# A one-core hybrid decoder step: the expert stage as 67 blocks of one expert each, or as 35 turns of a streamed and a resident block

## The chip, the core and the metric

The kernel runs on one core of a Trainium2 chip, in one launch. The metric is the device time of that core in microseconds (us). Everything is computed in float32.

## What is computed

One layer of a decoder: a prompt of 256 tokens and 8 samples of 4 tokens, so 288 tokens of width 1024. Modulation, input projection, dilated attention (the samples over cached keys and values) and a short convolution come first. The change is in the mixture of experts behind them: 32 experts, each token goes to the four with the highest logits, and each expert is a clamped SwiGLU layer with three 1024x1024 matrices.

```python
logits = xt @ w_router + b_router
top_v, top_i = lax.top_k(logits, TOP_K)          # 4 of 32
gates = jax.nn.softmax(top_v, axis=-1)
...
def expert_block(args):
    xblk, e = args
    g = xblk @ w_gate[e] + b_gate[e]
    u = xblk @ w_up[e] + b_up[e]
    g = jnp.minimum(g, SWIGLU_LIMIT)
    u = jnp.clip(u, -SWIGLU_LIMIT, SWIGLU_LIMIT)
    act = (u + 1) * g * jax.nn.sigmoid(SWIGLU_ALPHA * g)
    return act @ w_down[e] + b_down[e]
...
y = segment_sum(yb * row_g[:, None], row_tok)    # gated rows are added to their tokens
```

## The kernel before

Five programs run side by side, one for each engine, and wait for each other by semaphores written out by hand; nothing is scheduled for them. The input projection, attention and output projection use a ring of 12 slots (`ring`), each a weight piece of 128x2048 float32, 1 MB. Router, tables and experts follow.

**Blocks.** The rows that go to one expert are cut into blocks of 32 (`ROWS`). There are always `NB` = 288x4/32 + 31 = 67 blocks, in the order of the experts: each expert has one for every 32 rows begun, and experts with one block get an empty second one while blocks are left. An expert's weights are 12 pieces of 1 MB: four of w_gate (GATE), four of w_up (UP), four of w_down (DOWN). Every expert is loaded once, 384 pieces in all.

**A block on TensorE (PE), `moe_block`.** `biases` starts the sums in banks 0 and 1 with the owning expert's biases; `weights` runs the GATE pieces, then UP, then DOWN. A piece is 8 matmuls of 32 rows by 256 columns, four side by side in the array (16 records of the trace, since float32 makes two of one). Between them stand `combine(b - 1, h)`, which spreads the gated rows of the last block over the 288 token columns in two halves, `gather(b + 1)`, which picks the next block's 32 rows out of `h2tok` by a one-hot matrix, and the transposes `act_rows_T` (L892) and `gather_T` (L862).

**The other engines in a block.** VectorE (DVE) clips gate (L1304) and up (L1308), multiplies gate by its sigmoid (L953, two SBUF operands) and by up (L1316, two SBUF operands), writes the gated one-hot (L1289) and adds each combined half to `acc` (L953, 128x1152, 1.35 us). ScalarE (ACT) does the sigmoid and copies gathered and transposed rows out of PSUM.

**Loading.** All weight DMAs are issued by SyncE (SP) on one queue. UP and DOWN pieces, and expert 0's GATE pieces, go straight into the ring slot of their piece when the last block of the expert before has used it (`weights_used`). GATE pieces of the other experts go into four slots of `stage`, and GpSimd (POOL) copies them into the ring in two halves of 128x1024 (L479, L480), without a wait between the halves. So while one expert is computed, 16 pieces can be loaded or under way: 12 in the ring and 4 in the stage. Expert 0's 12 pieces and expert 1's GATE pieces are loaded during attention and the output projection (`EARLY` and what follows it). TensorE reads the block's expert from a table (`blk_e`).

## Time and profile before

| | us |
|---|---|
| median of 3 runs (1657.16 to 1665.85) | 1664.88 |
| the profiled execution | 1660.6 |
| its span, first to last instruction | 1658.5 |
| PE busy (matmul) | 1462.2 (88%) |
| DVE busy | 522.7 (32%) |
| ACT busy | 245.4 (15%) |
| POOL busy | 260.9 (16%) |
| DMA | 495.72 MB, mean 299 GB/s |
| granted TensorE clock, mean | 0.929 of 2.4 GHz |

The page puts 59% of the chain that ended last on the matmul helper's line L499 and 17% on transfers of w_gate and w_down. The expert blocks run from 428.3 us to about 1638.2 us of the span; the tables are ready at about 408.8 us. Shares of the whole span say little here, since the stages have different limits: in the page's 40 slices DMA stands at 400 GB/s and more in some slices of the expert stage and at 0 in others. "Records" below are the trace's matmul instructions.

### The profile page before, as it was taken

Reading aid. Unit: us, or ns where it says so; the run is one execution under the profiler, and the core shown is the slowest. Engines: PE = TensorE matmul, PEld = TensorE weight load, DVE = VectorE, ACT = ScalarE, POOL = GpSimd, SP = SyncE. Lnnn points to the kernel's source line nnn. Section 1 sums busy time; section 2 is a strip of 40 time slices with the busy share of each in tenths; the row PEclk is TensorE's granted clock in tenths of the full one; section 3 lists DMA queues with packets and bytes.
Section 4 is the critical chain, followed back from the end, with each engine's and each line's share of the span. In section 5 each row is a group of like instructions: output and inputs, shape, how many; then the busy total and the mean of one; then the engine's idle time right before and its main releaser. Section 6 shows DMA issues by size and latency. Waiting matters only on the chain.

```text
span 1658.5 us, 48934 instructions
## 1 busy us (share of the span) xinstructions
PE 1462.2 (88%) x20629; PEld 802.8 (48%) x20630; DVE 522.7 (32%) x1107; ACT 245.4 (15%) x639; POOL 260.9 (16%) x270
## 2 busy tenths in 40 slices
PE   6998999886999999999999997987689996776896
PEld 3885576563445555554555553532245552222353
DVE  2224445335223333333323332321123321121234
ACT  2113433311111111011111110100011110000011
POOL 0000000000211122123103111111300112312110
PEclk9998899897799999999999998988799998777898
DMA  9956989623196999999939969299960569999805
GB/s 338 370 219 227 335 314 344 236 94 127 56 400 250 406 404 401 407 405 399 405 125 382 404 256 410 87 411 409 410 266 0 206 256 409 410 410 409 328 25 207
DMA packets 143136, 495.72 MB, mean 299 GB/s; under 512 B 9069, under 2 KB 26085, under 8 KB 140030
## 3 DMA queue, kind: packets, MB, share of 16 engines
q1 hardware_dynamic: 141902, 491.00, 76.0%
q0 software_dynamic: 1200, 4.23, 0.7%
q8 instruction: 26, 0.43, 0.1%
q14 instruction: 8, 0.07, 0.0%
HBM read 492.22 MB, written 2.97 MB: 299 GB/s over the span
## 4 chain that ended last, share of the span: by engine, by line
PE 63%; DMA 20%; SPq 6%; DVE 5%; issue 3%; ACT 2%; POOL 1%; POOLq 0%; DVEq 0%; ACTq 0%
PE ps L499 59%; DMA arena<-in_w_gate 12%; DMA ring<-in_w_down 5%; SPq L405 5%; DMA arena<-in_cache_k 2%; PE ps L673 1%; PE ps L862 1%; DVE hT L953 1%; ACT hT L1525 1%; SPq L361 1%; POOL ring L480 1%; DVE arena L1289 1%; DVE hT L1308 1%; PE ps L514 0%; PE ps L648 0%
## 5 line engine op out<-in xcount | busy, mean ns | idle before, releaser
L499 PE MATMUL ps<-ring,hT 128*32 128x256 f32 (+2 forms) x13728 | 869.5, 389 | 101.9 <-POOL ring L480 51.7
L499 PEld LDWEIGHTS ps<-ring,hT 128*32 128x32 f32 (+1 forms) x13728 | 464.1, 114 | 471.4 <-issue 89.8
L499 PE MATMUL ps<-arena 128*32 128x258 f32 (+6 forms) x4252 | 258.6, 369 | 24.0 <-ACT arena L1459 3.7
L479 POOL COPY ring<-arena 128x1024 f32<-128x1024 f32 x124 | 129.0, 1040 | 941.1 <-PE ps L499 684.4
L1304 DVE TENSOR_SCALAR hT<-ps 128x256 f32<-128x256 f32 x67 | 28.4, 424 | 648.1 <-PE ps L499 648.1
L499 PEld LDWEIGHTS ps<-arena 128*32 128x32 f32 (+4 forms) x4252 | 129.0, 115 | 137.6 <-issue 93.5
L953 DVE TENSOR_TENSOR arena<-arena,ps 128x1152 f32<-128x1152 f32 x134 | 180.5, 1347 | 30.9 <-PE ps L499 30.9
L480 POOL COPY ring<-arena 128x1024 f32<-128x1024 f32 x124 | 131.3, 1059 | 0.0
L499 PE MATMUL ps<-arena,hT 32*128 32x288 f32 x1072 | 109.2, 478 | 2.0 <-DVE arena L953 1.5
L1525 ACT COPY hT<-ps 128x258 f32<-128x258 f32 x67 | 25.1, 375 | 440.6 <-PE ps L499 314.8
L1534 ACT ACTIVATE hT<-hT 128x256 f32<-128x256 f32 x67 | 27.9, 417 | 395.5 <-DVE hT L1304 395.5
L1308 DVE TENSOR_SCALAR hT<-ps 128x256 f32<-128x256 f32 x67 | 28.4, 424 | 181.3 <-PE ps L499 181.3
L499 PEld LDWEIGHTS ps<-arena,hT 32*128 32x128 f32 x1072 | 44.1, 193 | 64.5 <-issue 61.6
L1542 ACT COPY hT<-ps 128x256 f32<-128x256 f32 x67 | 24.9, 372 | 247.4 <-PE ps L499 247.4
L499 PE MATMUL ps<-hT,ring 128*128 128x288 f32 x224 | 56.5, 416 | 4.5 <-DVE hT L1173 3.4
L673 PE MATMUL ps<-ident,arena 128*128 128x128 f32 x336 | 49.8, 291 | 4.1 <-DMA arena<-in_cache_k 3.6
L499 PEld LDWEIGHTS ps<-hT,ring 128*128 128x128 f32 x224 | 43.5, 195 | 17.2 <-issue 5.0
L1357 ACT COPY arena<-ps 32x64 f32<-32x64 f32 (+6 forms) x91 | 31.7, 356 | 132.8 <-PE ps L499 101.6
L673 PEld LDWEIGHTS ps<-ident,arena 128*128 128x128 f32 x336 | 38.1, 147 | 14.9 <-issue 9.6
L862 PE MATMUL ps<-ident,hT 128*128 128x128 f32 x134 | 29.6, 303 | 13.7 <-ACT hT L1525 7.9
L1101 DVE COPY arena<-ps 128x512 f32<-128x512 f32 x40 | 27.7, 692 | 40.8 <-PE ps L673 40.8
L953 DVE TENSOR_TENSOR hT<-hT 128x256 f32<-128x256 f32 x67 | 39.6, 591 | 0.0
(191 smaller groups left out, 631.7 us busy)
## 6 DMA issues: line engine op xcount, KB each, us to landing
ring<-in_w_up SPq DMA_DIRECT2D x128, 1024.0 KB, 10.1
ring<-in_w_down SPq DMA_DIRECT2D x128, 1024.0 KB, 13.1
arena<-in_w_gate SPq DMA_DIRECT2D x124, 1024.0 KB, 18.1
ring<-in_w_ada SPq DMA_DIRECT2D x24, 1024.0 KB, 8.3
arena<-in_cache_k SPq DMA_DIRECT2D x56, 384.0 KB, 6.8
arena<-in_cache_v SPq DMA_DIRECT2D x56, 384.0 KB, 5.0
ring<-in_w_in SPq DMA_DIRECT2D x12, 1024.0 KB, 12.0
ring<-in_w_out SPq DMA_DIRECT2D x4, 1024.0 KB, 8.6
```

Of the source, the lines that this page charges most:

```text
L405: sp.dma_start(dst, src.rearrange("o (k p) c -> p (o k) c", p=P)).then_inc(signal, 16)
L479: pool.tensor_copy(slot[:, 0:half], stage[:, j, 0:half])
L480: pool.tensor_copy(slot[:, half:], stage[:, j, half:]).then_inc(staged_out, 1)
L499: return te.matmul(out, a, b, start=first, stop=last)
L673: last = tr(ps[:, b + hp // 4, (hp % 4) * P:(hp % 4 + 1) * P], K[:, c, hp * P:(hp + 1) * P], ident[:, :])
L862: last = tr(ps[:, 3, c * P:(c + 1) * P], xrows[:, c * P:(c + 1) * P], ident[:, :])
L953: return ve.tensor_tensor(out, a, b, op)
L1304: ve.tensor_scalar(tg, ps[:, 0, 0:256], LIMIT, None, ALU.min).then_inc(g_clipped, 1)
L1308: ve.tensor_scalar(tu, ps[:, 1, 0:256], LIMIT, -LIMIT, ALU.min, ALU.max).then_inc(u_clipped, 1)
L1357: return step(se.copy(out, in_), signal)
L1525: se.copy(xrows, ps[:, 3, 0:GW]).then_inc(x_copied_rows, 1)
L1534: se.activation(sg, tg, ACT.Sigmoid, scale=ALPHA).then_inc(g_sig, 1)
```

## The change

The 67 blocks become 35 turns (`TURNS`) of two blocks each (`PAIR`), 70 blocks. The first block of a turn is **streamed**: its 12 pieces come through the four stage slots, all twelve, and TensorE reads them there. The second is **resident**: its weights stand in the ring's 12 slots, where GpSimd puts them. GpSimd copies every piece of every turn out of the stage, in two halves. If the streamed expert is "heavy" (over 32 rows), the copy goes into the ring slot of the piece, and this expert's further blocks are the resident ones of this and the next turns. If it is "light", the copy goes to a spare place behind the ring (`SPILL`, 128x1024 float32, in `mem`), by an address computed from a register. Heavy experts are put at the turns where their further blocks begin, light ones at the turns that are left. Each turn streams 12 pieces whatever the routing, 420 in all.

A stage slot is free when TensorE has used it for the streamed block (`piece_used[0]`) and GpSimd has copied it (`held_in`); SyncE waits for both. Each GpSimd copy waits for the one before it (`held_in`). TensorE goes piece by piece: streamed piece j, then resident piece j, and the latter waits for GpSimd's copy of piece j in this turn. Biases, gather, transposes and combine are done for two blocks at a time; `combine` adds both blocks of a turn in PSUM, so the number of 128x1152 additions on VectorE stays two a turn. `actT` goes through banks 4 and 5, which `combine` uses too, so `act_rows_T` waits for the addition (`acc_added`). Nothing is loaded ahead any more: every expert DMA follows the tables. The bias sums of `b_down`, before ahead of the first block, stand inside turn 0. The tables themselves are made by other small steps.

```diff
@@ program, SyncE
-            for j in range(EARLY):
-                sp.wait_ge(pieces_used, FRONT_PIECES - SLOTS + 1 + j)
-                expert_piece(0, j)
...
-            for j in range(EARLY, EXP_PIECES):
-                sp.wait_ge(pieces_used, FRONT_PIECES - SLOTS + 1 + j)
-                expert_piece(0, j)
-            sp.wait_ge(o_copied, 2 * HPS * NSEQ)
-            for j in range(STAGES):
-                expert_piece(1, j)
+            def turn(t):
+                at = exp_row[0:1, t:t + 1] if isinstance(t, int) else exp_row[0:1, ds(t, 1)]
+                e = sp.value_load(at.bitcast(I32), min_val=0, max_val=NEXP - 1)
+                for j in range(EXP_PIECES):
+                    if not isinstance(t, int) or EXP_PIECES * t + j >= STAGES:
+                        sp.wait_ge(piece_used[0], EXP_PIECES * t + (j - STAGES + 1))
+                        sp.sem_inc(wait_passed, 1)
+                        sp.wait_ge(held_in, 2 * EXP_PIECES * t + 2 * (j - STAGES + 1))
+                        sp.sem_inc(wait_passed, 1)
...
+                    sp.dma_start(stage[:, j % STAGES, :].rearrange("p (k c) -> p k c", c=D),
+                                 src.rearrange("o (k p) c -> p (o k) c", p=P)).then_inc(stage_in[j % STAGES], 16)
@@ GpSimd
-                for j in range(STAGES):
-                    pool.wait_ge(stage_in[j], 16 * e)
-                    pool.wait_ge(weights_used, before * EXP_PIECES + (j + 1))
...
-                    pool.tensor_copy(slot[:, 0:half], stage[:, j, 0:half])
-                    pool.tensor_copy(slot[:, half:], stage[:, j, half:]).then_inc(staged_out, 1)
+                for j in range(EXP_PIECES):
+                    pool.wait_ge(stage_in[j % STAGES], 48 * t + 16 * (j // STAGES + 1))
+                    if not isinstance(t, int) or t > 0:
+                        pool.wait_ge(piece_used[1], EXP_PIECES * t + (j - EXP_PIECES + 1))
+                    for h in range(2):
+                        if not isinstance(t, int) or t > 0 or j > 0 or h > 0:
+                            pool.wait_ge(held_in, 2 * EXP_PIECES * t + (2 * j + h))
+                        pool.sem_inc(wait_passed, 1)
+                        home = j * PIECE + h * SPILL
+                        pool.tensor_copy(mem[:, ds(light * (SLOTS * PIECE - home) + home, SPILL)],
+                                         stage[:, j % STAGES, h * SPILL:(h + 1) * SPILL]).then_inc(held_in, 1)
@@ TensorE
+            def piece(b, j, i, x, bank):
+                if i == 0:
+                    te.wait_ge(stage_in[j % STAGES], 48 * b + 16 * (j // STAGES + 1))
+                    W = stage[:, j % STAGES, :].rearrange("p (k c) -> p k c", c=D)
+                else:
+                    te.wait_ge(held_in, 2 * EXP_PIECES * b + 2 * (j + 1))
+                    W = slot_w(j, rows=True)
...
+            def turn(b, first=False, last=False):
...
+                biases()
+                for u, pieces in enumerate((GATE, UP)):
+                    for j in pieces:
+                        for i in range(PAIR):
+                            piece(b, j, i, xe, 2 * u)
+                    if first:
+                        bias_sums(u)
+                    else:
+                        combine(b - 1, u)
...
+                        gather(b + 1, i)
...
+                    act_rows_T(b, i)
...
+                        gather_T(b + 1, i)
+                for j in DOWN:
+                    for i in range(PAIR):
+                        if j == DOWN[0]:
+                            te.wait_ge(actT_ready, 2 * b + (i + 1))
+                        piece(b, j, i, actT, 4)
@@ VectorE, in turn(b)
+                for i in range(PAIR):
+                    ve.wait_ge(glu, 2 * b + (i + 1))
+                    ve.wait_ge(u_clipped, 2 * b + (i + 1))
+                    ve.scalar_tensor_tensor(tu[i], tu[i], 1.0, sg[i], ALU.add, ALU.mult).then_inc(act_ready, 1)
+                total(b, 1, first)
                 gated_rows(b)
```

How the instructions stand, first on GpSimd in the loop over experts before. `ISA` and `REGISTER_ALU` are register steps; pure semaphore steps are not printed.

```order
24 L474 REGISTER_ALU
25 L475 ISA [waits stage_in0]
26 L479 COPY ring<-arena 128x1024 [waits weights_used]
27 L480 COPY ring<-arena 128x1024
28 L475 REGISTER_ALU [waits stage_in1]
29 L479 COPY ring<-arena 128x1024 [waits weights_used]
30 L480 COPY ring<-arena 128x1024
```

And on GpSimd in the loop over turns of the changed kernel, the first piece and the head of the second (a turn has twelve such).

```order
77 L466 ISA [waits stage_in0]
78 L469 REGISTER_ALU [waits piece_used1]
79 L472 ISA [waits held_in]
80 L472 COPY mem<-arena 128x1024
81 L469 REGISTER_ALU
82 L472 ISA [waits held_in]
83 L472 COPY mem<-arena 128x1024
84 L466 REGISTER_ALU [waits stage_in1]
85 L469 REGISTER_ALU [waits piece_used1]
```

Eight copies an expert became 24 a turn, and between any two of them there is now a wait for the earlier one and a register step for the address.

TensorE before, from the end of a block's UP pieces to its first DOWN piece:

```order
484 L499 MATMUL ps<-ring,hT 32x256 [waits piece_in11]
485 L499 MATMUL ps<-ring,hT 32x256 x7
486 L900 REGISTER_ALU
487 L499 MATMUL ps<-arena,hT 128x288 [waits acc_added]
488 L499 MATMUL ps<-arena,hT 128x288 x3
489 L851 ISA
490 L499 MATMUL ps<-arena 32x258 [waits hot_ready]
491 L499 MATMUL ps<-arena 32x258 x11
492 L892 MATMUL ps<-ident,hT 128x128 [waits act_ready]
493 L892 MATMUL ps<-ident,hT 128x128
```

The same place in a turn of the changed kernel (`arena` in a weight matmul is the stage, `mem` the ring):

```order
530 L499 MATMUL ps<-mem,hT 32x256 [waits held_in]
531 L499 MATMUL ps<-mem,hT 32x256 x7
532 L900 REGISTER_ALU
533 L499 MATMUL ps<-arena,hT 128x288 [waits acc_added]
534 L499 MATMUL ps<-arena,hT 128x288 x7
535 L847 ISA
536 L849 REGISTER_ALU [waits hot_ready]
537 L499 MATMUL ps<-arena 32x259 [waits u_clipped]
538 L499 MATMUL ps<-arena 32x259 x11
539 L499 MATMUL ps<-arena 32x259 [waits u_clipped]
540 L499 MATMUL ps<-arena 32x259 x11
541 L888 REGISTER_ALU
```

The stretch has twice the matmuls, its last UP piece waits for GpSimd instead of for a DMA, and the first transpose behind it (row 542 of that list) waits for `acc_added` and `act_ready`.

## Rows read from the trace of the kernel before

**Rows 1.** Two stretches: us, busy us (count) by engine, PEclk, DMA share, GB/s.
```profile
1140.00:1171.00 31.00, 21.69 (x252) 8.44 (x252) 5.07 (x10) 1.86 (x5) 8.34 (x9) 0.78 1.03 410
1235.00:1296.00 61.00, 60.50 (x1011) 31.85 (x1006) 19.59 (x40) 7.49 (x20) 0.00 (x0) 1.00 0.00 0
```

**Rows 2.** Timeline of PE over a block with no wait: start us, us, instruction.
```profile
1233.16 3.66 PE L499 MATMUL ps<-ring,hT 128*32 128x256 f32 x64
...
1241.78 3.66 PE L499 MATMUL ps<-ring,hT 128*32 128x256 f32 x64
1245.37 0.77 PE L499 MATMUL ps<-arena,hT 32*128 32x288 f32 x8
1246.06 1.51 PE L499 MATMUL ps<-arena 128*32 128x258 f32 x24
1247.51 0.44 PE L892 MATMUL ps<-ident,hT 128*128 128x128 f32 x2
...
1248.48 1.72 PE L499 MATMUL ps<-ring,hT 128*32 128x256 f32 x28
```

**Rows 3.** DMA issues of L405 in the stretch 351 to 375.3 us, each alone in its queue.
```profile
DMA to landing us min/median/max: 4.7/4.8/4.9
```

**Rows 4.** Chain of waits, from a landed stage piece to its copy, and from PE's use to the next DMA.
```profile
1107.27 0.02 issue
1107.30 0.03 POOLq L475
1107.33 0.04 issue
1107.37 0.02 POOLq L476
1107.39 0.11 issue
1107.51 0.06 POOL ring L479
...
1109.58 1.89 PE ps L499 x16
1111.47 0.08 SPq L405
...
1111.85 2.12 SPq L405
```

**Rows 5.** Timeline: two VectorE steps under GpSimd's copies, then the copies of one piece.
```profile
484.63 1.04 POOL L479 COPY ring<-arena 128x1024 f32<-128x1024 f32 x1 [0.47 <-DMA arena<-in_w_gate]
484.70 1.24 DVE L953 TENSOR_TENSOR hT<-hT 128x256 f32<-128x256 f32 x1
485.61 1.23 POOL L480 COPY ring<-arena 128x1024 f32<-128x1024 f32 x1
485.98 1.14 DVE L1316 SCALAR_TENSOR_TENSOR hT<-hT 128x256 f32<-128x256 f32 x1
...
1168.94 1.04 POOL L479 COPY ring<-arena 128x1024 f32<-128x1024 f32 x1 [0.54 <-DMA arena<-in_w_gate]
...
1169.93 1.04 POOL L480 COPY ring<-arena 128x1024 f32<-128x1024 f32 x1
...
1171.02 1.51 PE L499 MATMUL ps<-ring,hT 128*32 128x256 f32 x12 [0.62 <-POOL ring L480]
```

**Rows 6.** Timeline of VectorE between two blocks' UP and DOWN pieces, no copy running.
```profile
1245.50 0.42 DVE L1308 TENSOR_SCALAR hT<-ps 128x256 f32<-128x256 f32 x1 [2.15 <-PE ps L499]
1245.84 0.42 DVE L953 TENSOR_TENSOR hT<-hT 128x256 f32<-128x256 f32 x1
1246.30 0.42 DVE L1316 SCALAR_TENSOR_TENSOR hT<-hT 128x256 f32<-128x256 f32 x1
1246.64 0.43 DVE L1289 TENSOR_SCALAR arena<-arena,hT 128x288 f32<-128x288 f32 x1
...
1247.06 1.34 DVE L953 TENSOR_TENSOR arena<-arena,ps 128x1152 f32<-128x1152 f32 x1
```

**Rows 7.** Timeline at the start of the expert stage.
```profile
413.97 4.20 PE L499 MATMUL ps<-arena 32*128 32x288 f32 x8 [1.68 <-DVE arena L1268]
...
423.76 0.20 PEld L499 LDWEIGHTS ps<-arena 128*32 128x32 f32 x8 [0.76 <-issue]
...
426.63 0.37 ACT L1525 COPY hT<-ps 128x258 f32<-128x258 f32 x1 [17.01 <-PE ps L499]
...
428.31 1.11 PE L499 MATMUL ps<-arena 32*32 32x256 f32 x16 [0.55 <-ACT hT L1529]
...
429.35 8.37 PE L499 MATMUL ps<-ring,hT 128*32 128x256 f32 x128
```

**Rows 8.** Chain of waits at the end of the expert stage.
```profile
1637.08 1.11 PE ps L499 x16
...
1638.22 0.38 ACT hT L1542
...
1641.72 1.36 DVE arena L953
```

More of the change, by code:

```diff
@@ L838, in _, with gather @@
+                last = mm(ps[0:tn, 5, 256 + NB * t:256 + NB * (t + 1)], GT[0:NEXP, t0:t0 + tn], own2[0:NEXP, :], True, True)
             step(last, places_T)
-            te.wait_ge(place_ready, 3)
-            for h in range(2):
+            def gather(b, i):
+                if i == 0:
+                    te.wait_ge(hot_ready, 2 * b + 2)
+                if not isinstance(b, int) or b > 0:
+                    te.wait_ge(u_clipped, 2 * b + (i - 1))
+                for t in range(3):
+                    for q in range(4):
+                        last = mm(ps[q * 32:(q + 1) * 32, 2 + i, 0:GW], hot[:, t, i * ROWS:(i + 1) * ROWS], h2tok[:, t, q, :],
+                                  t == 0, t == 2)
+                last.then_inc(x_made, 1)
@@ new lines, in biases, with act_rows_T @@
+            def biases():
+                for q in range(4):
+                    for i in range(PAIR):
+                        for u in range(2):
+                            r = slice((2 * i + u) * NEXP, (2 * i + u + 1) * NEXP)
+                            mm(ps[32 * q:32 * q + 32, 2 * u + i, 0:256], own_b[r, :], brow[r, q * 256:(q + 1) * 256], True, False)
+            def act_rows_T(b, i):
+                te.wait_ge(act_ready, 2 * b + (i + 1))
+                if i == 0:
+                    te.wait_ge(acc_added, 2 * b + 2)
+                for c in range(2):
+                    last = tr(ps[:, 4 + i, c * P:(c + 1) * P], tu[i][:, c * P:(c + 1) * P], ident[:, :])
+                last.then_inc(act_T, 1)
@@ new lines, in combine @@
+            def combine(b, h):
+                if h == 0:
+                    te.wait_ge(ye_ready, 2 * b + 2)
+                    te.wait_ge(hotg_ready, 2 * b + 2)
+                te.wait_ge(acc_added, 2 * b + 2 + h)
+                for i in range(PAIR):
+                    for q in range(4):
+                        last = mm(ps[:, 4 + q, 0:NT], ye[i][32 * q:32 * q + 32, h * P:(h + 1) * P], hotg[i][32 * q:32 * q + 32, :],
+                                  i == 0, i == 1)
+                last.then_inc(comb_made, 1)
@@ L909, in moe_block @@
-            def moe_block(b, first=False, last=False):
-                at = blk_e[0:1, b:b + 1] if isinstance(b, int) else blk_e[0:1, ds(b, 1)]
-                e = te.value_load(at.bitcast(I32), min_val=0, max_val=NEXP - 1)
-                te.wait_ge(xe_ready, b + 1)
+            for i in range(PAIR):
+                gather(0, i)
+            for i in range(PAIR):
+                gather_T(0, i)
+            def turn(b, first=False, last=False):
+                te.wait_ge(xe_ready, 2 * b + 2)
@@ new lines, in turn @@
+                for i in range(PAIR):
+                    ve.wait_ge(g_sig, 2 * b + (i + 1))
+                    TT(sg[i], sg[i], tg[i], ALU.mult).then_inc(glu, 1)
+                total(b, 0, first)
+                for i in range(PAIR):
+                    ve.wait_ge(piece_used[i], EXP_PIECES * b + 8)
+                    if not first:
+                        ve.wait_ge(act_T, 2 * b + (i - 1))
+                    ve.tensor_scalar(tu[i], ps[:, 2 + i, 0:256], LIMIT, -LIMIT, ALU.min, ALU.max).then_inc(u_clipped, 1)
@@ new lines, in copy_x, with turn @@
+            def copy_x(b):
+                for i in range(PAIR):
+                    se.wait_ge(xT_made, 2 * b + (i + 1))
+                    se.copy(xe[i], ps[:, 2 + i, 0:256]).then_inc(xe_ready, 1)
+            def turn(b, first=False, last=False):
+                for i in range(PAIR):
+                    se.wait_ge(g_clipped, 2 * b + (i + 1))
+                    if not first:
+                        se.wait_ge(act_ready, 2 * b + (i - 1))
+                    se.activation(sg[i], tg[i], ACT.Sigmoid, scale=ALPHA).then_inc(g_sig, 1)
@@ L1544, in _ @@
             copy_rows(0)
             copy_x(0)
-            moe_block(0, first=True)
-            with se.Fori(1, NB - 1) as b:
-                moe_block(b)
-            moe_block(NB - 1, last=True)
+            turn(0, first=True)
+            with se.Fori(1, TURNS - 1) as b:
+                turn(b)
+            turn(TURNS - 1, last=True)
             load_sqrt()
```

397 lines of the change are left out of this document (177 added, 220 removed).

## The prediction

> **What bounds the kernel now.** I read the rates of stretches first, then the timeline of one block, then the chain of waits. A block that waits for nothing takes 15.32 us of TensorE, from the first DOWN matmul at 1233.16 to the next block's at 1248.48 [rows 2]; 67 of them would be 1026 us. The expert stage, from 428.31 to 1638.19 us, takes 1210 [rows 7, 8]. The 184 us between are waits for weights. They fall where experts have one block each: between 1140 and 1171 us DMA runs at 410 GB/s, TensorE holds 252 matmul records in 31 us and its granted clock averages 0.78 of 2.4 GHz. Where one expert has many blocks it is the other way: from 1235 to 1296 us DMA moves nothing and TensorE holds 1011 records in 61 us at clock 1.00 [rows 1]. So two resources take turns at being the bound. A piece of 1.049 MB takes 2.56 us at 410 GB/s, an expert's twelve 30.7 us, two blocks 30.6 us. The change lays the two side by side; at best a turn would cost 30.7 us and 35 turns 1075 us. The question is what a turn really costs.
>
> **The period of a turn.** Four stage slots set a loop. Next turn's GATE piece 0 needs the slot of this turn's DOWN piece 0, and TensorE reads DOWN piece 0 only after the long gap between UP and DOWN. I follow this loop from the moment F when GpSimd ends the last copy of UP piece 3.
>
> - TensorE starts the resident UP piece 0.05 us after that copy (the copy ends at 1170.97, TensorE starts at 1171.02) [rows 5]. The piece costs 0.90 us, a quarter of the 3.59 us between 1241.78 and 1245.37 [rows 2]. F + 0.95.
> - `combine` was 0.69 us, 1245.37 to 1246.06 [rows 2]. With twice the records it costs between 0.69 and 1.38; I take 1.2, since the switch between shapes is paid once. F + 2.15.
> - Two gathers at 1.45 us each, 1246.06 to 1247.51 [rows 2]: F + 5.05.
> - The transposes of one block and what they wait for took 0.97 us, 1247.51 to 1248.48 [rows 2], two blocks' between 0.97 and 1.94: DOWN begins at F + 6.0 to 7.0. VectorE may be later than that: from F + 1.05 on it has a clip (0.42), two products, which took 0.42 each alone and 1.14 to 1.24 while GpSimd copied, the addition (1.34), and two gated one-hots (0.43) before ScalarE may copy rows and then `actT` (0.38 each) [rows 5, 6, 8]. With one product free and one held that is 1.05 + 0.42 + 0.42 + 1.14 + 1.34 + 0.86 + 0.76 = 6.0, with both held 6.8. I take F + 6.5.
> - The streamed DOWN piece 0 ends 1.1 us later [rows 8], SyncE's steps up to the issue took 0.38 us (1111.47 to 1111.85) [rows 4], and a DMA alone in its queue took 4.7 to 4.9 us to land [rows 3]: F + 12.8. During the gap the four DOWN pieces fill the slots, DMA stands still for some 2 to 3 us, and nothing later gives them back.
> - From landing to GpSimd's copy 0.24 us (1107.27 to 1107.51) [rows 4]: F + 13.0.
> - Then sixteen copies for GATE and UP. A copy took 1.04 us [rows 5]. Before, the second half began 0.99 us after the first; now each waits for the one before. No row of before shows such a wait on GpSimd. Its pieces are there: 0.05 us until a waiter sees the copy's end [rows 5], 0.02 + 0.11 us from the semaphore step to the copy, 0.03 us for a register step and 0.04 behind it [rows 4]. That is 0.27 us with the gaps, so 1.31 us a copy. The bounds are 1.24 (the address step hidden) and 1.45 (it costs several such steps). 16 x 1.31 - 0.27 = 20.7: F + 33.7.
> - VectorE's steps with two SBUF operands hold GpSimd up in return: a copy with such a step ahead took 1.23 us, 0.19 more [rows 5]. Three fall among these sixteen copies (two gate products, the one-hot): 0.6.
>
> The period is **34.3 us**: more than DMA's 30.7, and more than GpSimd's 24 x 1.31 = 31.4. TensorE itself has about 29 us of work in it (six times 3.6 for weights, then 2.4, 2.9, 2 and under 1 for biases), so it isn't the bound.
>
> The Trainium skill, "SBUF — State Buffer", section "Who interferes with whom", says that a VectorE instruction with two SBUF inputs and a GpSimd instruction that reads SBUF exclude each other for a whole instruction. The trace agrees, with 1.24 against 0.42 us for one product [rows 5, 6]; without that rule's cost the period would be about 33.3, by the same rows.
>
> **Start and end.** Attention doesn't change: the loads taken out of it were issued where the queue was waiting for TensorE. The tables take about as many steps as before, so I leave 413.97 as the moment when they stand [rows 7]; the small added steps, 0.2 us each, are about balanced by dropped ones. The bias sums (413.97 to 423.76) move into turn 0, where loading covers them. Then 0.4 for the one-hot, two gathers at 2.87 (423.76 to 426.63, low clock), 2.4 for copies and transposes of two blocks (1.68 for one), twice 1.04 for biases, and 1.9 for GATE piece 0 at the low clock: 426.5 [rows 4, 7]. The first four pieces have landed by then. UP piece 0 is issued and lands 5.2 later, and four pieces of copies (0.24 + 8 x 1.31 - 0.27) end at about 442: this is F of turn 0. With expert 0 no longer loaded ahead, this fill is the price at the front. After the last F: DOWN begins about 5.5 later (no gather), its eight pieces take 7.2, the tail from 1638.19 to the end of the span took 20.3 [rows 8] and has two longer combines, 0.5 each: 34.0.
>
> Sum: 442 + 34 x 34.3 + 34.0 = 1642 us of span, against 1658.5. The profiled execution was 2.1 us over its span and the median of the runs 4.3 us over that, so the median after should be **1648 us**, 1.0% less. Each 0.1 us of the period is 3.4 us of time. The time is unchanged at a period of 34.8; faster by over 0.5% below 34.5, slower by over 0.5% above 35.0 (about what a measurement of this kernel can tell from no change).
>
> **Rivals.**
>
> *Loading sets the pace (0.24).* If the copies go at 1.24 us, eight landings at 2.56 us rule: 12.8 + 17.9 + 0.24 + 2.45 = 33.4, and 32.9 with the shortest gap. The time would be 442 + 34 x 33.2 + 34 + 6.4 = 1611 us. For it: the copies' bound is only 5% away. Against it: sixteen copies are then within 0.1 us of loading, with VectorE pushing them.
>
> *GpSimd's copies cost more, slower than before (0.25).* If a dependent copy with a register address costs 1.45 us, sixteen cost 22.9 and the period is 36.5: 1723 us. It decides from 1.36 us a copy on, since 13.0 + 16 x 1.36 - 0.27 + 0.6 = 35.1. For it: no row shows such a copy, 24 of them follow one another, and VectorE now has five two-operand steps a turn in place of two a block. Against it: the steps visible in rows 4 are short.
>
> *The clock falls (0.05).* Between 1140 and 1171 us the clock averaged 0.78 while TensorE held 8.1 records a us [rows 1]. Were the gap between UP and DOWN at 1.2 GHz, combine, gathers, transposes and DOWN piece 0 would cost twice, some 6 us more: a period of 40 and about 1850 us. Against it: a turn has 504 records in 34.3 us, 14.7 a us, much nearer to the 16.6 of the stretch at 1.00. The Trainium skill, "TensorE: Matmul & The Clock Gate", Part 1, says that the clock is throttled by default and released by activity; that waiting lowers it agrees with the 0.78 here.
>
> *The change does all it says (0.04).* If the stage covered the gap, a turn would cost 30.7 us: 442 + 34 x 30.7 + 40.4 = 1526 us. Against it stands the loop above: the slot isn't free.
>
> **How the numbers follow.** The forecast has 0.42; its own range is a period of 33.8 to 34.9, 1632 to 1669 us. About 0.25 of it lies on the faster side of 0.5%, 0.11 within and 0.06 beyond. With the rivals: faster 0.25 + 0.24 + 0.04 = 0.53, within 0.5% 0.11, rounded to 0.12, slower 0.06 + 0.25 + 0.05, so 0.35. The range leaves out the full cover, the low clock and the dear end of the copies: 1598 to 1715 us.
>
> **What would show it.** Twelve pieces every 34.3 us, DMA at about 370 GB/s with one pause a turn, at the GATE pieces; GpSimd copies starting 1.31 us apart in GATE and UP, idle for about 2 us before GATE piece 0; TensorE's resident pieces released by GpSimd; clock 1.00 through the turns. Wrong would be: copies over 1.36 us apart, a chain that runs through GpSimd without passing the DMA of GATE piece 0, or a first F later than 445 us.

## The result, and the profile after

The changed kernel took 1671.35 us (median of 20 runs, 1661.08 to 1685.33), the kernel before 1658.98 (20 runs, 1653.78 to 1671.55): ratio 1.0065, 95% interval 1.0046 to 1.0083. The forecast was 1648 and "faster". The time lies in the range, on the other side of no change.

The page of the kernel after: span, clock, transfer rate, the chain that ended last, and the group of GpSimd's copies.

```profile
span 1671.0 us, 54045 instructions
...
PEclk9998899997999999999999999999999999999998
...
GB/s 337 371 213 238 122 320 347 217 24 74 327 369 369 370 330 363 369 368 365 331 370 361 363 360 350 342 371 353 364 371 309 351 370 357 368 359 345 366 366 158
...
POOL 40%; PE 23%; DMA 19%; issue 8%; DVE 4%; POOLq 4%; SPq 1%; ACT 1%; DVEq 0%; ACTq 0%
...
L472 POOL COPY mem<-arena 128x1024 f32 x840 | 899.3, 1071 | 408.1 <-POOL mem L472 195.6
```

TensorE's granted clock is 0.99 of 2.4 GHz on the mean of the turns, where it had averaged 0.78 in the loading stretches [rows 1], and DMA runs from the first turn to the last, at 357 GB/s on the mean (row below). So the change did what its structure says. F, the end of UP piece 3's copies, is at 438.98 us in turn 0 and at 1637.07 in turn 34: 34 periods of 35.24 us. Two stretches of the kernel after (us, busy us (count) by engine, clock, DMA share, GB/s), the standstill in one turn, and all turns:

```profile
973.20:976.20 3.00, 3.00 (x54) 1.80 (x58) 0.00 (x0) 1.01 (x4) 2.49 (x3) 1.00 0.15 36
...
438.98:1637.07 1198.09, 1015.02 (x17128) 527.28 (x17128) 305.45 (x508) 116.74 (x340) 874.54 (x818) 0.99 0.92 357
```

One turn, whose F is at 966.85. First TensorE's timeline (start us, us, instruction, wait ahead), which answers to [rows 2]: resident UP piece 3, combine, gathers, transposes, then DOWN, streamed (`arena`) and resident (`mem`) by turns.

```profile
966.90 1.07 PE L499 MATMUL ps<-mem,hT 128*32 128x256 f32 x16 [0.65 <-POOL mem L472]
967.90 1.25 PE L499 MATMUL ps<-arena,hT 32*128 32x288 f32 x16
969.08 2.83 PE L499 MATMUL ps<-arena 128*32 128x259 f32 x48
...
973.16 0.44 PE L860 MATMUL ps<-ident,arena 128*128 128x128 f32 x2 [0.44 <-ACT arena L1561]
973.53 1.07 PE L499 MATMUL ps<-arena,hT 128*32 128x256 f32 x16
974.41 1.05 PE L499 MATMUL ps<-mem,hT 128*32 128x256 f32 x16
```

Then VectorE between the same pieces, which answers to [rows 6], with ScalarE's copy of the second gather's rows, which waits for the one-hots; and SyncE's issues of the next GATE pieces:

```profile
968.38 1.59 DVE L1354 SCALAR_TENSOR_TENSOR mem<-mem 128x256 f32<-128x256 f32 x2
969.89 1.34 DVE L971 TENSOR_TENSOR arena<-arena,ps 128x1152 f32<-128x1152 f32 x1
971.16 1.48 DVE L1318 TENSOR_SCALAR arena<-arena 128x288 f32<-128x288 f32 x2
972.73 0.38 ACT L1561 COPY arena<-ps 128x259 f32<-128x259 f32 x1 [0.75 <-DVE arena L1318]
```
```profile
975.01 5.48 SPq L426 DMA_DIRECT2D arena<-in_w_gate  x4
```

Last GpSimd's copies from the end of DOWN on, which answer to [rows 5]:

```profile
976.72 1.04 POOL L472 COPY mem<-arena 128x1024 f32 x1 [0.25 <-POOL mem L472]
980.25 1.04 POOL L472 COPY mem<-arena 128x1024 f32 x1 [2.49 <-DMA arena<-in_w_gate]
981.55 1.04 POOL L472 COPY mem<-arena 128x1024 f32 x1 [0.26 <-POOL mem L472]
983.52 1.04 POOL L472 COPY mem<-arena 128x1024 f32 x1 [0.93 <-DMA arena<-in_w_gate]
984.81 1.04 POOL L472 COPY mem<-arena 128x1024 f32 x1 [0.25 <-POOL mem L472]
...
991.27 1.04 POOL L472 COPY mem<-arena 128x1024 f32 x1 [0.25 <-POOL mem L472]
992.57 1.30 POOL L472 COPY mem<-arena 128x1024 f32 x1 [0.25 <-POOL mem L472]
```

And the chain of waits for GATE 1, from its issue over its landing to its first copy:

```profile
976.78 6.34 DMA arena<-in_w_gate
...
983.15 0.03 POOLq L466
...
983.22 0.03 POOLq L469
...
983.30 0.02 POOLq L470
...
983.38 0.06 POOLq L472
...
983.51 0.03 POOLq L469
983.54 1.03 POOL mem L472
```

The loop of the prediction is all there. DOWN begins 6.7 us behind F in this turn, and on the median of the turns too. GATE 0 is issued at 8.2 and first copied at 13.4, after an idle 2.49 us. Copies then follow 1.29 us apart (1.04 and a pause of 0.25). The row that the forecast doesn't have is the one at 983.52: GpSimd stands idle a second time, 0.93 us, for GATE 1, whose load took 6.34 us.

### The profile page after: what moved, and what is told of

It is laid out like the page before. It is cut to its first block, busy times and chain, and to the rows that moved or that the text cites. A ratio compares the mean times of both kernels' runs of the same rounds, so it can differ in the third digit from the quotient of the medians.

```text
span 1671.0 us, 54045 instructions
## 1 busy us (share of the span) xinstructions
PE 1410.4 (84%) x21389; PEld 804.2 (48%) x21389; DVE 488.1 (29%) x970; ACT 241.7 (14%) x654; POOL 910.3 (54%) x864
## 4 chain that ended last, share of the span: by engine, by line
POOL 40%; PE 23%; DMA 19%; issue 8%; DVE 4%; POOLq 4%; SPq 1%; ACT 1%; DVEq 0%; ACTq 0%
POOL mem L472 40%; PE ps L499 20%; DMA arena<-in_w_gate 14%; DMA arena<-in_cache_k 2%; POOLq L472 2%; DMA arena<-in_w_up 2%; PE ps L673 2%; DVE arena L971 1%; SPq L372 1%; POOLq L469 1%; DVE arena L1318 1%; POOLq L470 1%; DMA arena<-in_w_down 0%; PE ps L514 0%; PE ps L648 0%
## 5 line engine op out<-in xcount | busy, mean ns | idle before, releaser
L472 POOL COPY mem<-arena 128x1024 f32 x840 | 899.3, 1071 | 408.1 <-POOL mem L472 195.6
L499 PE MATMUL ps<-mem,hT 128*32 128x256 f32 (+2 forms) x7584 | 522.1, 372 | 171.0 <-POOL mem L472 168.8
L499 PE MATMUL ps<-arena,hT 128*32 128x256 f32 (+1 forms) x7840 | 530.7, 389 | 5.7 <-DMA arena<-in_w_gate 3.3
L499 PEld LDWEIGHTS ps<-mem,hT 128*32 128x32 f32 (+1 forms) x7584 | 257.4, 113 | 401.4 <-POOL mem L472 283.2
L499 PEld LDWEIGHTS ps<-arena,hT 128*32 128x32 f32 (+1 forms) x7840 | 258.1, 121 | 205.6 <-issue 64.9
L499 PE MATMUL ps<-arena 128*32 128x259 f32 (+5 forms) x4376 | 220.6, 360 | 17.8 <-ACT arena L1493 3.7
L499 PEld LDWEIGHTS ps<-arena 128*32 128x32 f32 (+3 forms) x4376 | 121.6, 112 | 102.1 <-issue 55.0
L971 DVE TENSOR_TENSOR arena<-arena,ps 128x1152 f32<-128x1152 f32 (+1 forms) x71 | 94.1, 1325 | 10.5 <-PE ps L499 10.4
L499 PE MATMUL ps<-hT,mem 128*128 128x288 f32 x224 | 56.5, 416 | 4.5 <-DVE hT L1191 3.4
L1354 DVE SCALAR_TENSOR_TENSOR mem<-mem 128x256 f32<-128x256 f32 x70 | 53.9, 812 | 0.0
```

The source lines that it names most:

```text
L472: pool.tensor_copy(mem[:, ds(light * (SLOTS * PIECE - home) + home, SPILL)], stage[:, j % STAGES, h * SPILL:(h + 1) * SPILL]).then_inc(hel ...
L499: return te.matmul(out, a, b, start=first, stop=last)
L971: return ve.tensor_tensor(out, a, b, op)
L1354: ve.scalar_tensor_tensor(tu[i], tu[i], 1.0, sg[i], ALU.add, ALU.mult).then_inc(act_ready, 1)
```

## The experiments

The period is the distance from the F of turn 0 to that of turn 34, over 34. Columns: median (the two kernels with half of the copies have one run), ratio to the kernel before with its interval, period, and, behind F on the mean of 32 turns, when GATE 0 is issued and first copied.

| kernel | median us | ratio | period | issue | copy |
|---|---|---|---|---|---|
| after | 1671.35 | 1.0065 [1.0046, 1.0083] | 35.24 | 8.15 | 13.50 |
| e1 half of the copies | 1597.63 | | 33.25 | | |
| e2 streamed DOWN first | 1648.75 | 0.9917 [0.9892, 0.9941] | 34.37 | 8.17 | 13.52 |
| e3 combine early | 1614.68 | 0.9716 [0.9666, 0.9766] | 33.60 | 6.19 | 11.83 |
| e4 e3, streamed DOWN 0 ahead | 1636.65 | 0.9851 [0.9808, 0.9894] | 34.03 | 4.41 | 11.63 |
| e5 e2 and e3 | 1578.75 | 0.9509 [0.9485, 0.9533] | 32.57 | 6.19 | 11.55 |
| e6 e4 in another order | 1603.03 | 0.9671 [0.9643, 0.9698] | 33.06 | 4.70 | 11.79 |
| e7 e6, half of the copies | 1525.50 | | 30.83 | | |
| e8 e6, half loads | 1583.77 | 0.9564 [0.9539, 0.9588] | 32.60 | 4.22 | 11.37 |
| e9 e5, half loads | 1583.05 | 0.9558 [0.9526, 0.9591] | 32.61 | 6.23 | 11.18 |
| e10 gathers in UP | 1578.90 | 0.9535 [0.9510, 0.9560] | 32.55 | 5.93 | 11.22 |
| e11 e5, two spill places | 1554.51 | 0.9381 [0.9352, 0.9410] | 31.77 | 6.19 | 11.56 |
| e12 e10, two spill places | 1570.97 | 0.9479 [0.9449, 0.9510] | 32.18 | 6.55 | 10.71 |
| e13 e11, half loads | 1556.79 | 0.9368 [0.9314, 0.9422] | 31.91 | 6.23 | 10.70 |

**e1, half of the copies.**
```diff
-                    for h in range(2):
+                    for h in range(1):
```


> The kernel after, but GpSimd copies only the first half of each piece (12 copies a turn in place of 24), so the resident block works with half of its weights left over from other data; loads, matmuls and waits are otherwise the same. The trace of after has a mean turn of 35.24 us from one end of the copies of UP's last piece (F) to the next. Theory A, the four-slot loop: the stretch from F to GATE0's landing (13.3 us) stays, since it goes through the combine, the gathers, the transposes and the first DOWN piece and holds no copy; behind it the pieces GATE0 to UP3 then come in at the pace of their loads, about 2.75 us each, 7 x 2.75 = 19.3, and one copy with its gap (1.3) ends the turn, less a few tenths that no longer collide: 33.3 us a turn, and a span of 439 + 34 x 33.3 + 34 = 1605 us. Theory B, GpSimd's 24 copies of a turn are themselves the bound, and the wait before GATE0 only looks like a cause: with 12 copies the turn falls to TensorE's own work, 30.7 us, and the span to about 1517 us. Theory C, the bare pace of the loads is the bound already: no change, 1671 us.

(The counts that SyncE, GpSimd and TensorE wait for are halved with it.) Measured: span 1595.7, period 33.25. GpSimd's copy count is halved and the period falls by 2 us only. GpSimd in one turn of e1:

```profile
944.19 1.04 POOL L472 COPY mem<-arena 128x1024 f32 x1 [3.09 <-DMA arena<-in_w_gate]
947.75 1.04 POOL L472 COPY mem<-arena 128x1024 f32 x1 [2.52 <-DMA arena<-in_w_gate]
950.26 1.04 POOL L472 COPY mem<-arena 128x1024 f32 x1 [1.47 <-PE ps L499]
952.82 1.04 POOL L472 COPY mem<-arena 128x1024 f32 x1 [1.52 <-PE ps L499]
```

From GATE 1 on the copies come 2.56 us apart, the pace of the loads at 410 GB/s. (TensorE, named as releaser, had used the place of that copy a turn before; the wait that ended last is the load.) In after two copies take 2.59. So loads and copies were about 1% apart behind GATE 1, and the stretch from F to GATE 0's copy, 13.3 us here and 13.5 in after, stays. Theory A holds; B would have had 30.7 and C no change. Its terms were others, though: not seven pieces at 2.75 us, but 3.4 us to GATE 1's copy and six at 2.56.

**e2, the streamed DOWN pieces first.**
```diff
-                for j in DOWN:
-                    for i in range(PAIR):
+                for i in range(PAIR):
+                    te.wait_ge(actT_ready, 2 * b + (i + 1))
+                    for j in DOWN:
```


> The kernel after, but TensorE takes the four streamed DOWN pieces first and the four resident ones after them, in place of one and one by turns; nothing else changes. In after GATE's loads are issued 1.78 us apart (8.16, 9.94, 11.64, 13.27 us behind F), because each waits for two DOWN pieces of TensorE; GATE1's copy starts 3.3 us behind GATE0's, where two copies take 2.58. Theory A: the issues of GATE1 to GATE3 come 0.9 us apart, GATE1 lands within the 2.6 us of GATE0's copies, the 16 copies from GATE0 to UP3 run without that pause, and the turn falls by 0.7 us to 34.5: span 439 + 34 x 34.5 + 34 = 1646 us, ratio to the kernel before about 0.992. Rival: four loads asked for almost at once share the queues, GATE0's landing is put off by what GATE1 gains, and the turn stays at 35.2: 1671 us.

Measured: 1648.75 us, 34.37 a turn. SyncE's four issues of GATE in a turn of e2, and GpSimd's copies:

```profile
937.32 3.38 SPq L426 DMA_DIRECT2D arena<-in_w_gate  x4
```
```profile
942.63 1.04 POOL L472 COPY mem<-arena 128x1024 f32 x1 [2.55 <-DMA arena<-in_w_gate]
943.93 1.04 POOL L472 COPY mem<-arena 128x1024 f32 x1 [0.26 <-POOL mem L472]
945.22 1.04 POOL L472 COPY mem<-arena 128x1024 f32 x1 [0.25 <-POOL mem L472]
```

The four issues take 3.38 us, where in after they took 5.48, and the second wait is gone: GATE 1's copy starts 2.59 us behind GATE 0's in nearly every turn, in place of 3.41 on the mean. GATE 0's isn't put off (13.52). The order in which the two blocks read DOWN cost 0.87 us a turn.

**e3, the combine early.** TensorE does `combine(b - 1, 1)` behind UP piece 1; VectorE its `total` and `gated_rows` before UP's clips.
```diff
-                    if first:
-                        bias_sums(u)
-                    else:
-                        combine(b - 1, u)
+                        if j in (GATE[3], UP[1]):
+                            if first:
+                                bias_sums(u)
+                            else:
+                                combine(b - 1, u)
...
                 total(b, 0, first)
+                total(b, 1, first)
+                gated_rows(b)
```


> The kernel after, but the second half of the previous turn's combine stands behind UP's second piece in place of behind its last, and VectorE does its sum and the gated one-hots ahead of UP's clips. TensorE's work between F and the first DOWN piece loses 1.2 us. Theory A, the four-slot loop runs through that stretch: DOWN0 begins 1.2 us earlier (5.3 us behind F in place of 6.5), so does GATE0's load, GpSimd's wait for it falls by 1.2 us, and the turn falls from 35.2 to 34.0: span 439 + 34 x 34.0 + 34 = 1629 us, ratio to the kernel before 0.982. Theory B or C (copies or the pace of the loads alone): no change, since all the work is still there, 1671 us.

Measured: 1614.68 us, 33.60, more than expected. GATE 0 is issued 1.96 us earlier, not 1.2: the sum and the one-hots (1.34 and 1.48 in the rows of after) had held ScalarE's copy of the gathered rows, and with it the transposes of x, too. TensorE in a turn of e3, with no wait behind resident UP 3:

```profile
912.44 1.07 PE L499 MATMUL ps<-mem,hT 128*32 128x256 f32 x16 [0.33 <-POOL mem L472]
913.33 2.81 PE L499 MATMUL ps<-arena 128*32 128x259 f32 x48
916.07 0.66 PE L892 MATMUL ps<-ident,mem 128*128 128x128 f32 x4
916.56 0.60 PE L860 MATMUL ps<-ident,arena 128*128 128x128 f32 x4
917.09 1.07 PE L499 MATMUL ps<-arena,hT 128*32 128x256 f32 x16
```

**e4, streamed DOWN 0 ahead of the gathers.**
```diff
                         for i in range(PAIR):
+                            if j == UP[3] and i == 1:
+                                act_rows_T(b, 0)
                             piece(b, j, i, xe, 2 * u)
...
+                piece(b, DOWN[0], 0, actT, 4)
                 if not last:
                     for i in range(PAIR):
                         gather(b + 1, i)
+                act_rows_T(b, 1)
+                piece(b, DOWN[1], 0, actT, 4)
```


> The change of e3, and with it the streamed block is carried through on its own: VectorE makes its product ahead of the resident block's clip, TensorE transposes it before the resident UP3 piece and takes the streamed DOWN0 piece ahead of the gathers and the streamed DOWN1 piece behind them; the resident block's transposes, the gathers' transposes and the rest follow. DOWN0 is then used about 1 us behind F in place of 7.6, and the load of GATE0 waits only for GpSimd's copy of DOWN0 (2.6 us behind F). Theory A: the slot loop is no longer the longest one and the pace of the loads sets the turn, 12 x 2.77 = 33.2 us: span about 439 + 34 x 33.2 + 34 = 1602 us, ratio to before 0.966. Theory B (GpSimd's copies are a bound of their own at 24 x 1.29 = 31 us, or longer where VectorE's steps lie over them): at most the same, it can't be told apart from A unless the turn stays above 34. Theory C: 1671 us, no change.

A miss: 34.03, worse than e3. TensorE in a turn of e4:

```profile
918.75 1.05 PE L499 MATMUL ps<-arena,hT 128*32 128x256 f32 x16
921.69 0.44 PE L892 MATMUL ps<-ident,mem 128*128 128x128 f32 x2 [1.90 <-DVE mem L1359]
922.06 1.07 PE L499 MATMUL ps<-mem,hT 128*32 128x256 f32 x16
922.95 1.05 PE L499 MATMUL ps<-arena,hT 128*32 128x256 f32 x16
923.81 2.81 PE L499 MATMUL ps<-arena 128*32 128x259 f32 x48
```

The transposes wait 1.90 us for the product, and resident UP 3, which could run from F on (920.07 in this turn), stands behind them until 922.06; over 1040 us that wait sums to 52.0 us. GATE 0 was issued at 4.4 and not 2.6, and GATE 1 at 8.5, behind both gathers. Of the 1.8 us by which GATE 0 is issued earlier than in e3, 0.2 are left at its first copy (11.63 against 11.83). An engine that executes in order pays for an early place of a step that isn't ready.

**e5, e2 and e3 together.** The diffs of both.

> The two edits of e2 and e3 together: the combine's second half behind UP's second piece, and the four streamed DOWN pieces ahead of the resident ones. In e3 GATE0's first copy starts 11.7 us behind F (13.5 in after) and GATE1's 3.3 us behind it; in e2 that pause is gone (2.59). Theory A, the slot loop with GpSimd's 16 copies at its end: both gains add, GATE0's copy at 11.8 and 16 copies in 20.7 us give a turn of 32.5 us and a span of 439 + 34 x 32.5 + 34 = 1578 us, ratio to before 0.951. Rival: the loads have a floor of their own near 33 us a turn (e1, with half of the copies, ended at 33.25): 439 + 34 x 33.2 + 34 = 1602 us. The records speak for 2.56 us a piece, 30.7 us a turn, which would leave theory A its room.

Measured: 1578.75 us; 32.57 a turn. The gains add (0.87 + 1.64 = 2.51, measured 2.67), and no floor near 33 us shows.

**e6, the order of e4 mended.** Resident UP 3, transposes of block 0, gather, streamed DOWN 0 and 1, gather, transposes of block 1, and the rest.

> The pieces of e4 in another order on TensorE, with VectorE and ScalarE as in e4: resident UP3, transposes of the streamed product, gather of the first block, streamed DOWN0 and DOWN1, gather of the second block, transposes of the resident product, streamed DOWN2, the gathers' transposes, resident DOWN0, streamed DOWN3, resident DOWN1 to DOWN3. In e4 TensorE stood before the resident UP3 piece until VectorE had clipped and multiplied the streamed block, and streamed DOWN1 came only behind both gathers, so GATE0's load was asked for at 4.3 us and GATE1's at 8.4 us behind F. Theory A: here DOWN0 is used 3.5 us behind F and DOWN1 4.4, DOWN1's load has landed by then, so GATE0 is asked for at 3.9 us and GATE1 at 5.2, the queues never run dry, and the turn is set by GpSimd's own 24 copies, 31.0 us and some tenths of collisions: 31.5 us, span 439 + 34 x 31.5 + 34 = 1544 us (0.931). Rival: TensorE, with 30.7 us of work in a turn, is now the late engine wherever it waits once for a product or a copy, and gives 1 to 2 us of that back, as in e4: 32.5 to 33.5 us, 1578 to 1612 us.

A miss on the time, the rival: 33.06. TensorE's wait for the product is down to 13.0 us in 1040, but GATE 0, issued at 4.7, is copied at 11.8 only, and the loads run at 381 GB/s with nothing standing still.

**e7, e6 with half of the copies.** The diff of e1 on e6.

> The kernel of e6 with the edit of e1: GpSimd copies only the first half of each piece, so the resident block works in part with left-over weights. It tells which engine bounds e6. If GpSimd's copies bound e6, the turn falls to the loads' and TensorE's floor, 30.7 us, and the span to 1517 us. If TensorE's waits for products bound e6, it gains only what shorter copies give on the way (1.3 us for the one copy behind UP3): about 1 us a turn less than e6.

Measured: 1525.50 us, 30.7 in nearly every turn (30.83 with the first): 12 loads at 2.56. TensorE's order doesn't bound e6; GpSimd's copies and the slots that they hold do.

**e8, half loads on e6.** Each piece is loaded in two halves with a signal each, and a half is asked for when the half in its place is copied.
```diff
-                        sp.wait_ge(held_in, 2 * EXP_PIECES * t + 2 * (j - STAGES + 1))
+                            sp.wait_ge(held_in, 2 * EXP_PIECES * t + 2 * (j - STAGES) + h + 1)
```


> The kernel of e6, but each piece is loaded in two halves of 512 KB with a signal each, and a half is asked for as soon as GpSimd has copied the half that lay there (SyncE still waits for TensorE once a piece). In e6 nothing runs dry any more, yet the turn is 33.06 us where the loads alone need 12 x 2.56 = 30.7 and GpSimd alone 24 x 1.295 = 31.1. Theory S, the slots: with one of four slots held for 2.6 us by its two copies, at most three loads are on the way; a load behind two others takes 3 x 2.56 = 7.7 us, and a slot's round is 7.7 + 2.6 + 0.4 + waits = 10.8 us, three rounds a turn 32.3 to 33. With halves 3.5 pieces are on the way, the round shrinks by 1.3 us, and the turn falls to GpSimd's 31.4: span 439 + 34 x 31.4 + 34 = 1541 us. Theory T, TensorE's own waits for products set the turn of e6: no change, 1596 to 1603 us.

Measured: 1583.77 us, 32.60, every turn but the first at 32.6. No load is waited for any more, but a copy now also waits for its own half's signal, behind the wait for its predecessor, and the pause grew:

```profile
902.70 1.04 POOL L475 COPY mem<-arena 128x1024 f32 x1 [0.28 <-POOL mem L475]
904.02 1.04 POOL L475 COPY mem<-arena 128x1024 f32 x1 [0.28 <-POOL mem L475]
...
908.09 1.04 POOL L475 COPY mem<-arena 128x1024 f32 x1 [0.39 <-POOL mem L475]
```

24 copies of 1.04 are 25.0 us, 23 pauses of 0.28 (five of 0.33) 6.7, the head of the turn 0.4 and copies lengthened by VectorE 0.5: 32.6. This is GpSimd alone as the bound. The slots' share of e6 was real (nothing waits for a load now), its worth was 0.5 us before the next bound.

**e9, half loads on e5.** The diff of e8 on e5.

> The kernel of e5 with the half loads of e8. In e5 GATE0 is asked for 6.2 us behind F, its first copy starts at 11.5 to 11.6, and 16 copies of 20.7 us follow: 32.5 us. Here the first copy needs only the first half of GATE0's load; estimated from the records, a 1 MB load alone takes 4.8 us and 2.56 us of that is its bytes at the pace of the queues, so half of it takes 4.8 - 1.3 = 3.5. Slot loop: the first copy starts 1.3 us sooner, but GpSimd's eight DOWN copies end only at 10.6, so the turn falls from 32.5 to GpSimd's own 31.4: 1541 us, ratio to before 0.929. Rival: twice as many loads cost SyncE and the queues more than they give (24 x 0.4 us of issue, a pause between loads), and the turn stays at 32.5 or rises: 1579 us or more.

Measured: 1583.05 us, 32.61: nearly the same bound. The first copy comes 0.37 us earlier than in e5, but most pauses are 0.03 us longer and five are 0.08 us longer. The expectation priced the extra wait at nothing.

**e10, gathers in UP.** On the kernel of e8, with its half loads and its order of DOWN.
```diff
+                        if j == UP[2] and not last:
+                            for i in range(PAIR):
+                                gather(b + 1, i)
```


> The half loads of e8 and the early combine of e3, and the gathers of the next blocks are moved too: behind UP's third piece, into the two banks that GATE's sums have left, with their copies by ScalarE; behind F remain resident UP3, the transposes, and DOWN, whose first streamed piece then begins about 2.6 us behind F in place of 4.7. Theory A: GATE0 is asked for by 4 us behind F, nothing but GpSimd's copies is left in the loop, 31.4 us a turn, 1541 us, the same as e9 if that reaches the floor; if e9 doesn't reach it, this one is nearer. Rival: TensorE has nothing left to do while it waits for the products (clip, product, transposes, copy: some 1.5 us), so its own 29.6 us of work and this wait give 31.1 us with no slack, and the turn comes out at 32 us or more: 1561 us.

Measured: 1578.90 us, 32.55. The gathers now stand before UP 3 on TensorE: in one turn streamed UP 3 starts 1.25 us behind F and resident UP 3 2.1. Moving 2.8 us of work out of one gap put it ahead of the pieces that open the next. GATE 0 is issued at 5.93, not 4. That isn't what sets this turn, though: of 1040 us GpSimd waits 3.7 us for loads and 2.8 us for TensorE, and its 24 copies with pauses of 0.28 to 0.33 us fill the turn as in e8. That pause is what the expectation's 31.4 us left out.

**e11, two places for the spilled copies.** With one place each spilled copy writes what the copy before it wrote, so it waits for that one. With two, by turns, it waits for the copy before the last.
```diff
-                            pool.wait_ge(held_in, 2 * EXP_PIECES * t + (2 * j + h))
+                            pool.wait_ge(held_in, 2 * EXP_PIECES * t + (2 * j + h) - 1)
...
-                        pool.tensor_copy(mem[:, ds(light * (SLOTS * PIECE - home) + home, SPILL)],
+                        pool.tensor_copy(mem[:, ds(light * (SLOTS * PIECE + h * SPILL - home) + home, SPILL)],
```


> The kernel of e5, but what GpSimd copies for light experts goes to two places by turns in place of one (four small tiles of VectorE and ScalarE move to make room), so a copy waits for the copy before the last, which has long ended, and no longer for its predecessor. Work, loads and order are the same. In after as in e5 a copy of 1.04 us is followed by 0.25 us in which GpSimd waits for its own signal; in e8 to e10, with one more wait per copy, that pause is 0.28 to 0.33 and the turn stands at 32.5 us although no load and no matmul is waited for. Theory G, this pause is a part of the bound: it falls by 0.15 to 0.2 us, 16 copies from GATE0 on take about 18 us in place of 20.7, but then they wait for the loads, 2.56 us a piece: 11.5 + 7 x 2.56 + 2.3 = 31.7 us a turn, span 439 + 34 x 31.7 + 34 = 1551 us, ratio to before 0.935. Rival: the pause is GpSimd's own start-up of a copy (its address is read from a register) and not the wait: it stays, and so does the turn, 32.5 us, 1579 us.

Measured: 1554.51 us, 31.77. GpSimd in a turn of e11, and its chain:

```profile
936.54 2.02 POOL L477 COPY mem<-arena 128x1024 f32 x2 [1.32 <-DMA arena<-in_w_gate]
939.05 2.02 POOL L477 COPY mem<-arena 128x1024 f32 x2 [0.48 <-DMA arena<-in_w_gate]
941.61 2.02 POOL L477 COPY mem<-arena 128x1024 f32 x2 [0.54 <-DMA arena<-in_w_gate]
```
```profile
DMA 56%; PE 20%; issue 8%; POOL 7%; DVE 3%; POOLq 2%; SPq 2%; ACT 1%; DVEq 0%; ACTq 0%
```

Two copies in 2.02 us: the pause was wholly the wait for the own signal, and its 0.25 us is gone, start-up and address step included. Copies now start 2.56 us apart, at the pace of the loads, and the chain, 40% GpSimd in after, is 56% DMA. 11.56 + 7 x 2.56 + 2.1 = 31.6.

**e12, the same on e10** (so with half loads).

> The same edit on the kernel of e10, in which GATE0's load is asked for early and nothing but GpSimd's copies bounds the turn (32.5 us = 24 copies of 1.32 and 0.8 us at the head of a turn). Theory G: with a pause of about 0.1 us they need 24 x 1.14 + 0.8 = 28.2 us, and the loads bound the turn at 12 x 2.56 = 30.7 us, as in e7: span 439 + 34 x 30.8 + 34 = 1520 us, ratio 0.916. Rival (the pause is GpSimd's start-up): no change, 32.4 us a turn, 1577 us.

A miss: 1570.97 us, 32.18. The pause is gone as a bound, but TensorE is still late at UP 3, GATE 0 is issued at 6.55, and the records of the queues show 277 to 361 GB/s from 7 to 13 us behind F.

**e13, half loads on e11.**

> The kernel of e11 with the half loads of e9. In e11 a turn is 11.5 us from F to GATE0's first copy and then 7 pieces at the pace of the loads and two copies, 31.6 us. The stretch from GATE0's issue (6.2 us behind F) to its first copy, 5.3 us in after and in e2, e5 and e11, is a term of the sum that came out 0.3 us too small. If it is the whole load that the copy waits for, half a load frees the first copy about 1 us sooner: 10.6 us behind F (e9's was held by GpSimd's DOWN copies, which in e11 end at 10.1), then 15 half pieces at 1.28 us and one copy of 1.04: 30.9 us a turn, span 439 + 34 x 30.9 + 34 = 1524 us, ratio to before 0.919. If most of the 5.3 us is a fixed delay of a load and not its bytes, the first copy stays at 11.2 or later and the turn at 31.5: 1545 to 1555 us.

Measured: 1556.79 us, 31.91. The first copy did move, from 11.56 to 10.70 behind F: the half load lands 4.21 us after its issue where the whole one took 4.97, and the copy follows 0.26 us later in place of 0.40. So the load's bytes count in this term. The turn didn't follow: the second half is copied 1.5 us behind the first and the third 1.7 behind that, and the records of the queues show 266 to 376 GB/s from 7 to 13 us behind F, where e11 has 351 to 421 from 8 on. From 8 us on the other kernels with half loads dip too (at the lowest 266 GB/s in e8, 218 in e9, 194 in e10, 283 in e12). What slows eight small loads there stays open.

## Why the prediction was wrong

*The parts that held.* The bound was the one named: from F through the gap, the slot of DOWN 0 and the load of GATE 0 to sixteen copies. e3 and e5 shortened this loop and moved the time; e1 halved the copies and did little. F of turn 0 came at 439.0 (forecast 442), the end at 33.9 (34.0), DOWN at 6.7 (6.5), GATE 0's issue at 8.15 (8.0), the clock at 0.99 (1.00), a copy with its pause at 1.295 us (1.31). All four rivals fell: dependent copies don't come 1.45 us apart, loading alone didn't rule, the clock stood, and a turn costs 35.2 us and not 30.7. So the time did rise, but not by the rival that had it rise.

*The step that failed* is "then sixteen copies for GATE and UP". It took GATE 0's landing as the last wait of a turn and let the copies run through. Its own rule, a slot is asked for when TensorE has read the piece in it, holds for GATE 1 too. From the end of one streamed DOWN piece to the end of the next TensorE reads two pieces (1.78 us), so GATE 1 is issued 1.8 us behind GATE 0. It then takes 6.6 us to land on the mean, where GATE 0's load took 4.95. GpSimd is idle for it for 0.93 us in the turn shown, 0.68 more than its usual pause, and 0.82 more on the mean. The forecast said "one pause a turn"; there are two. e2 takes that order away alone, GATE 1's load takes 6.6 us there too, and the pause is gone: 34.37 us a turn, the forecast's 34.3. That its 1648.75 us also meet the forecast's 1648 is partly luck, since two terms outside the period were off and partly cancel: in e2's profile the F of turn 0 came at 446.2, where the forecast had 442, and the 6.4 us below weren't there.

One thing about this pause stays open. GATE 1 is issued 9.4 to 10.1 us behind F in all of the 32 turns, yet its load takes anything from 5.6 to 7.8 us, and GpSimd is idle for 0.25 to 2.2 us. With a load of 4.8 us, as the forecast had it for GATE 0, there would have been no pause. What makes this load longer, and by another amount in each turn, no run here tells.

*The terms that were mis-sized, and cancel.* A period of 35.16 (mean of turns 2 to 33) against 34.3:

| term | forecast | measured |
|---|---|---|
| F to GATE 0's issue | 7.98 | 8.15 |
| issue to first copy | 5.04 | 5.35 |
| sixteen copies | 20.7 | 16 x 1.295 - 0.25 = 20.47 |
| VectorE's collisions | 0.6 | 0.26 |
| GATE 1's pause | none | 0.82 |
| other waits | none | 0.1 |

The 5.35 are a load of 4.95 (forecast 4.8, from loads alone in their queue [rows 3]) and 0.40 from its landing to its copy (0.24, from a chain with two small steps of GpSimd's sequencer [rows 4], where there are now five, as the chain for GATE 1 shows). e2, with the next load 0.9 us behind in place of 1.8, shows the same 5.35. A copy that VectorE holds up costs more than the 0.19 put down, 1.30 in place of 1.04 at 992.57, but in the turn shown it is the only one of the sixteen, where the forecast had three.

*The front and the offset.* 34 x 0.94 = +32 us for the period and -3 for the start give the span: 1671.0 against 1642. The forecast then added 6.4 us for the distance from span to median, 4.3 of them from three runs whose median lay above the profiled one. Over 20 runs before's median is 0.5 us above its span; that term was 6 us too much and hid a part of the miss.

*The chances.* The forecast wrote that the time rises by over 0.5% from a period of 35.0 on, 0.7 us from its centre, and gave its own case 0.06 on that side. A sum of ten terms with one unexamined wait among them doesn't have that precision.

*Where the gain of the change went.* A turn has 30.7 us of loads and about as much of TensorE's work, yet takes 35.2. 1.6 us are the combine, the sum and the one-hots in the gap (e3), 0.9 the DOWN order (e2), 0.8 the wait of a copy for its predecessor (e11 against e5). With these three the same design runs at 1554.51 us, 6.2% under the kernel before.

The Trainium skill, "SBUF — State Buffer", section "Who interferes with whom", says that a VectorE instruction with two SBUF inputs contends with a GpSimd instruction that reads SBUF. The trace agrees in kind: the two products with both inputs in SBUF took 1.59 us beside copies, where one took 0.42 alone [rows 6], and copies took up to 1.30.

## What to carry to other kernels

When a slot loop bounds a period, follow every slot through it, not the first alone: the order in which a consumer alternates between two sources sets when the second and third slots come free. A copy whose result nobody reads still costs the wait for its place; a second place takes the wait away. Steps moved ahead of work that is ready, on an engine that executes in order, can cost more than the gap they leave (e4, e12).

## What was not expected of the hardware

A GpSimd copy of 128x1024 f32 that waits for the one before it costs 1.04 + 0.25 us; two that don't wait take 2.02 us together, address from a register included, so they overlap by 0.06 us. It matters where a further wait stands. In after a piece's first copy has two more waits than its second, ahead of the wait for the predecessor, and both pause 0.25 us; in e8 the wait for the half's signal stands behind it, and the pauses are 0.28 and 0.33. A load of 1 MB into an empty queue landed 4.95 us after its issue on the mean (after, e2), the one issued 0.9 or 1.8 us behind it 6.6 us after its own. In e7 loads ran at 410 GB/s over 960 us beside GpSimd's twelve copies a turn and TensorE at clock 1.00. VectorE's one-hot, with one SBUF input, took 0.78 us beside copies (0.43 alone [rows 6]): more than two-input steps are held up.
